# Five weight chunks of the mixer layer as ten chunks of 256 columns with two matmuls per tile, and ScalarE scaling the state-space output

## The reference, cut to what matters

```
proj = x @ w_in                                  # x: (256, 1024)
z, xbc, dt_raw = proj[:, :1024], proj[:, 1024:2560], proj[:, 2560:2576]
sc_b, sc_c, sc_h = the last three blocks of 1024 columns
xbc = silu(causal_dwconv(xbc, conv_w) + conv_b)  # 4 taps along the tokens
...                                              # scan over two blocks of 128 tokens, 16 heads
y_ssd = rms_norm_by_group(y * silu(z)) * norm_w  # 2 groups of 512 columns
y_sc  = sc_b * causal_dwconv(sc_c * sc_h, sc_conv_w)   # 3 taps
mix   = concatenate([y_ssd, y_sc]) @ w_out
```

## Time and profile before

| | |
|---|---|
| median of 3 runs | 1211.0 us (1210.92 to 1212.75) |
| the profiled execution, its own time | 1211.0 us |
| its span, first to last instruction | 1209.1 us |
| PE busy | 1202.8 us, 99% |
| PEld busy | 1043.0 us, 86% |
| DVE, ACT, POOL busy | 55%, 56%, 71% |
| the chain that ended last | PE 98% |
| granted TensorE clock | 1.000 |

### The profile page before, as it was taken

How to read it: one execution, slowest core, us unless ns; L and a number is a source line. 1 busy time by engine, 2 the same in 40 slices (tenths; PEclk the granted TensorE clock), 3 DMA queues, 4 the chain that set the end, 5 groups by cost and what they waited for, 6 DMA issues and landing times.

```text
span 1209.1 us, 18481 instructions
## 1 busy us (share of the span) xinstructions
PE 1202.8 (99%) x7352; PEld 1043.0 (86%) x7352; DVE 667.5 (55%) x1147; ACT 679.2 (56%) x913; POOL 855.8 (71%) x371
## 2 busy tenths in 40 slices
PE   9999999999999999999999999999999999999998
PEld 8987888888888888899999888888889878888887
DVE  6847546331256689646662255537753673544865
ACT  6873757655476755546544464445556666444543
POOL 7977468649978800968589788883776648998174
PEclk9999999999999999999999999999999999999999
DMA  9756355537656656746466766665657445666462
GB/s 303 214 161 174 107 155 157 157 89 222 211 151 197 190 164 217 215 130 192 124 178 216 251 200 189 182 197 164 224 147 279 140 121 173 186 202 189 160 223 70
DMA packets 147989, 218.32 MB, mean 181 GB/s; under 512 B 9792, under 2 KB 79808, under 8 KB 147904
## 3 DMA queue, kind: packets, MB, share of 16 engines
q1 hardware_dynamic: 144384, 209.92, 57.2%
q10 hardware_dynamic: 3520, 7.23, 1.7%
HBM read 216.08 MB, written 1.05 MB: 180 GB/s over the span
## 4 chain that ended last, share of the span: by engine, by line
PE 98%; DMA 0%; ACT 0%; DVE 0%; issue 0%; SPq 0%; DVEq 0%; ACTq 0%
PE acc L2285 18%; PE acc L2292 9%; PE acc L2322 9%; PE acc L2324 9%; PE acc L2323 9%; PE pm L2338 5%; PE acc L2329 4%; PE acc L2331 4%; PE acc L2332 4%; PE acc L2743 3%; PE acc L2744 3%; PE acc L2745 3%; PE acc L2251 2%; PE acc L2253 2%; PE acc L2252 2%; PE acc L2487 1%
## 5 line engine op out<-in xcount | busy, mean ns | idle before, releaser
L645 POOL TENSOR_TENSOR wlo<-raw,whi 128x1024 fp32r<-128x1024 f32 (+4 forms) x362 | 848.0, 2373 | 340.9 <-ACT whi L659 226.2
L659 ACT ACTIVATE whi<-raw 128x1024 fp32r<-128x1024 f32 (+4 forms) x404 | 403.7, 1022 | 210.9 <-PE acc L2292 54.0
L2285 PE MATMUL acc<-XT,whi 128*128 128x512 f32 x960 | 229.8, 391 | 0.4 <-DVE XT L1233 0.4
L2285 PEld LDWEIGHTS acc<-XT,whi 128*128 128x128 f32 x960 | 176.3, 188 | 35.2 <-issue 0.8
L2292 PEld LDWEIGHTS acc<-XT,wlo 128*128 128x128 f32 x960 | 123.4, 191 | 4.8
L2292 PE MATMUL acc<-XT,wlo 128*128 128x256 f32 x960 | 124.8, 283 | 0.0
L2322 PE MATMUL acc<-whi,XT 128*128 128x512 f32 (+4 forms) x296 | 112.5, 380 | 0.1
L2329 PE MATMUL acc<-XT,whi 128*128 128x256 f32 x392 | 111.7, 285 | 0.2 <-issue 0.2
L2331 PE MATMUL acc<-XT,whi 128*128 128x256 f32 x392 | 111.0, 283 | 0.0
L2332 PE MATMUL acc<-XT,wlo 128*128 128x256 f32 x392 | 111.0, 283 | 0.0
L2324 PE MATMUL acc<-whi,XT 128*128 128x512 f32 (+4 forms) x296 | 110.1, 372 | 0.0
(11 more groups left out here) (524 smaller groups left out, 2276.0 us busy)
## 6 DMA issues: line engine op xcount, KB each, us to landing
raw<-in_w_in SPq DMA_DIRECT2D x68, 512.0 KB, 3.9
raw<-in_w_ff SPq DMA_DIRECT2D x64, 512.0 KB, 3.8
raw<-in_w_gate SPq DMA_DIRECT2D x44, 512.0 KB, 3.8
raw<-in_w_up SPq DMA_DIRECT2D x44, 512.0 KB, 3.8
raw<-in_w_down SPq DMA_DIRECT2D x44, 512.0 KB, 3.9
raw<-in_w_in_mix SPq DMA_DIRECT2D x36, 512.0 KB, 3.8
raw<-in_w_branch SPq DMA_DIRECT2D x16, 512.0 KB, 3.8
raw<-in_w_out_mix SPq DMA_DIRECT2D x16, 512.0 KB, 3.4
```

The costliest lines, as they stand in the source:

```text
L645: nc.gpsimd.tensor_tensor(piece(wlo, u), piece(raw, u), piece(whi, u).bitcast(F32), ALU.subtract).then_inc(S["w_lo"], 1)
L659: return nc.scalar.activation(out_, in_, func, **k)
L2285: T.matmul(acc[:, n % 2, f, :], piece(whi, u)[:, i, f * P:(f + 1) * P], XT[:, :, k, :], start=k == 0, stop=False)
```

## The change

The chunks `xbc0`, `xbc1`, `sc1`, `sh1` and `sb1` are planned as ten "B" chunks of 256 columns, named `xbc00`, `xbc01`, `xbc10` and so on. The number of units stays the same. VectorE adds their partial sums in two new operations per chunk, the copy going into parts of the tile `em`. Each half is then convolved, multiplied and split by itself. At the start TensorE takes the first unit of `xbc01` between the two units of `xbc00`. ScalarE no longer copies `sc1`, VectorE's addition writes `scc`. The four scalings of `yd` go from VectorE to ScalarE, before the high halves of `sb0`'s result. The output products wait for their tiles by the finer count of `c_lo`.

```diff
+    def halves(name, at):
+        for h in range(2):
+            g.append((f"{name}{h}", "w_in_mix", KD, at + h * HW, HW, "B"))
...
-        g.append((f"xbc{c}", "w_in_mix", KD, M_XBC + c * W, W, "F"))
+        if c < 2:
+            halves(f"xbc{c}", M_XBC + c * W)
+        else:
+            g.append(("xbc2", "w_in_mix", KD, M_XBC + c * W, W, "F"))
...
-            g.append((f"{n}{c}", "w_in_mix", KD, o + c * W, W, "F"))
+            if c == 0:
+                g.append((f"{n}0", "w_in_mix", KD, o, W, "F"))
+            else:
+                halves(f"{n}1", o + W)
...
+        part_sums = em[:].rearrange("p h r s -> p h (r s)").rearrange("p h (f t) -> p h f t", t=TOK)
+        SHORT_OUT = (("sb0", slice(8, 12)), ("sb10", slice(12, 14)), ("sb11", slice(14, 16)))
...
 # ScalarE
-                act.wait_ge(*evac_at(f"xbc{j}"))
+                act.wait_ge(*evac_at(("xbc01", "xbc11", "xbc2")[j]))
...
-            for c in range(2):
-                if c:
-                    leave("sc1", scc[:])
-                high_halves(landed(f"sb{c}") + AHEAD)
-                act.wait_ge(S["c_out"], c + 1)
-                fn(BYhi[:, 8 + 4 * c:12 + 4 * c, :], accF(f"sb{c}"), ACT.Copy).then_inc(S["c_hi"], 1)
+            high_halves(landed("sb0") - 2 + AHEAD)
+            act.wait_ge(S["y_ss"], 2)
+            for k in range(4):
+                last = fn(y4[:, k, :], y4[:, k, :], ACT.Copy, scale=rs[:, k:k + 1])
+            last.then_inc(S["y_n"], 1)
+            for n, (name, tiles) in enumerate(SHORT_OUT):
+                high_halves(landed(name) + AHEAD)
+                act.wait_ge(S["c_out"], n + 1)
+                fn(BYhi[:, tiles, :], short_view(name), ACT.Copy).then_inc(S["c_hi"], 1)
...
 # VectorE
+            def parts_added(name, h, out_=None):
+                v.wait_ge(S["w_used"], landed(name))
+                link(V.tensor_copy(part_sums[:, h], accB(name, 1)))
+                return V.tensor_tensor(accB(name, 0) if out_ is None else out_, accB(name, 0), part_sums[:, h], ALU.add)
...
+            for j in range(3):
+                if j < 2:
+                    for h in range(2):
+                        link(parts_added(f"xbc{j}{h}", h))
+                        convolved(f"xbc{j}{h}", accB(f"xbc{j}{h}", 0), 4 * j + 2 * h)
...
-            for k in range(4):
-                last = V.tensor_scalar(y4[:, k, :], y4[:, k, :], rs[:, k:k + 1], None, ALU.mult)
-            last.then_inc(S["y_n"], 1)
-            short_output(0)
-            short_input(1)
-            short_output(1)
+            V.engine_nop().then_inc(S["y_ss"], 1)
+            v.wait_ge(S["w_used"], landed("sb0"))
+            short_output(0, "sh0", slice(0, 4))
+            for h in range(2):
+                parts_added(f"sc1{h}", h, scc[:, 2 * h:2 * h + 2]).then_inc(evac_at(f"sc1{h}")[0], 1)
+            for h in range(2):
+                v.wait_ge(*evac_at(f"sc1{h}"))
+                link(parts_added(f"sh1{h}", h))
+                short_input(f"sh1{h}", 1, slice(2 * h, 2 * h + 2))
+            for h in range(2):
+                link(parts_added(f"sb1{h}", h))
+                short_output(1 + h, f"sh1{h}", slice(2 * h, 2 * h + 2))
...
 # TensorE
-            product("xbc0", XThi, XTlo, 0, 1, ready=turned("x3"))
+            product("xbc00", XThi, XTlo, 0, 1, ready=turned("x3"))
             pe.wait_ge(*evac_at("f2_1"))
             turn("x3", X, first=2)
-            product("xbc0", XThi, XTlo, 1, ready=turned("x3"))
-            product("xbc1", XThi, XTlo)
+            product("xbc01", XThi, XTlo, 0, 1, used=0)
+            product("xbc00", XThi, XTlo, 1, ready=turned("x3"), used=2)
+            product("xbc01", XThi, XTlo, 1)
+            product("xbc10", XThi, XTlo)
+            product("xbc11", XThi, XTlo)
...
-            from_x("sc1")
-            from_x("sh1")
-            from_x("sb1")
+            for name in ("sc1", "sh1", "sb1"):
+                for h in range(2):
+                    from_x(f"{name}{h}")
...
-                product(name, BYhi[:, KD:], BYlo[:, KD:], start, stop, ready=lambda j: (S["c_lo"], j // 2 + 1))
+                product(name, BYhi[:, KD:], BYlo[:, KD:], start, stop, ready=lambda j: (S["c_lo"], max(1, j)))
```

More of the change, by code:

```diff
@@ L542, in accB, with short_view @@
             return acc[:, n % 2, 0:w // P, part * TOK:(part + 1) * TOK]
+        part_sums = em[:].rearrange("p h r s -> p h (r s)").rearrange("p h (f t) -> p h f t", t=TOK)
         f1s = pm[:, 3, :].rearrange("p (f t) -> p f t", t=TOK)
         hm = pm[:, 3, :].rearrange("p (f t) -> p f t", t=TOK)
+        y4 = yd[:].rearrange("p t (g d) -> p (t g) d", g=2)
+        SHORT_OUT = (("sb0", slice(8, 12)), ("sb10", slice(12, 14)), ("sb11", slice(14, 16)))
+        def short_view(name):
+            return accF(name) if chunks[name][5] == "F" else accB(name, 0)
         def last_gate(j):
@@ L991, in _ @@
             turn("x3", XThi, first=2)
-            high_halves(landed("xbc1") + AHEAD)
+            high_halves(landed("xbc11") + AHEAD)
             def silu2(j):
-                act.wait_ge(*evac_at(f"xbc{j}"))
+                act.wait_ge(*evac_at(("xbc01", "xbc11", "xbc2")[j]))
                 fn(xbcT[:, 4 * j:4 * j + 4, :], xbcT[:, 4 * j:4 * j + 4, :], ACT.Silu).then_inc(S["silu2"], 1)
@@ L1799, in by_head, with convolved @@
                 return ap.rearrange("p (h d) -> p h d", d=SSD_D)
-            for j in range(3):
-                v.wait_ge(S["w_used"], landed(f"xbc{j}"))
+            def parts_added(name, h, out_=None):
+                v.wait_ge(S["w_used"], landed(name))
+                link(V.tensor_copy(part_sums[:, h], accB(name, 1)))
+                return V.tensor_tensor(accB(name, 0) if out_ is None else out_, accB(name, 0), part_sums[:, h], ALU.add)
+            def convolved(name, view, first):
+                n = view.shape[1]
                 for back in range(4):
-                    for f in range(4 * j, 4 * j + 4):
-                        w, x = bcol("ssd_conv_w", 12 * (3 - back) + f), accF(f"xbc{j}")[:, f % 4, 0:TOK - back]
+                    for f in range(first, first + n):
+                        w, x = bcol("ssd_conv_w", 12 * (3 - back) + f), view[:, f - first, 0:TOK - back]
                         if back == 0:
@@ L1811, in _ @@
                         link(last)
-                last.then_inc(evac_at(f"xbc{j}")[0], 1)
+                last.then_inc(evac_at(name)[0], 1)
+            for j in range(3):
[3 more added lines that the diff above has]
+                        convolved(f"xbc{j}{h}", accB(f"xbc{j}{h}", 0), 4 * j + 2 * h)
+                else:
+                    v.wait_ge(S["w_used"], landed("xbc2"))
+                    convolved("xbc2", accF("xbc2"), 8)
                 if j == 1:
@@ L1854, in _, with short_input @@
             V.tensor_tensor(yd[:, 1, :], off, yd[:, 1, :], ALU.add).then_inc(S["s_yod"], 1)
[L1856 to L1861, removed]
+            def short_input(name, c, tiles):
+                gated = short_view(name)
+                link(V.tensor_tensor(gated, gated, scc[:, tiles], ALU.mult))
                 for back in range(3):
-                    for f in range(4):
+                    for f in range(tiles.start, tiles.stop):
                         w = bcol("sc_conv_w", 8 * (2 - back) + 4 * c + f)
-                        x = gated[:, f, 0:TOK - back]
+                        x = gated[:, f - tiles.start, 0:TOK - back]
                         if back == 0:
@@ L1872, in short_input, with short_output @@
                         link(last)
[L1873 to L1883, removed]
+                last.then_inc(evac_at(name)[0], 1)
+            def short_output(n, source, part):
+                name, tiles = SHORT_OUT[n]
+                view = short_view(name)
+                v.wait_ge(*evac_at(source))
+                V.tensor_tensor(view, view, scv[:, part], ALU.mult).then_inc(S["c_out"], 1)
+                v.wait_ge(S["c_hi"], n + 1)
+                V.tensor_tensor(BYlo[:, tiles, :], view, BYhi[:, tiles, :].bitcast(F32), ALU.subtract)\
+                    .then_inc(evac_at(name)[0], 1)
+                v.wait_ge(*evac_at(name))
                 V.engine_nop().then_inc(S["c_lo"], 1)
@@ L1923, in _ @@
             finished(3)
-            short_input(0)
+            v.wait_ge(S["w_used"], landed("sh0"))
+            v.wait_ge(*evac_at("sc0"))
+            short_input("sh0", 0, slice(0, 4))
             v.wait_ge(S["y_ss"], 1)
@@ L1927, in _ @@
             refine_columns(0, 4)
-            y4 = yd[:].rearrange("p t (g d) -> p (t g) d", g=2)
-            for k in range(4):
-                last = V.tensor_scalar(y4[:, k, :], y4[:, k, :], rs[:, k:k + 1], None, ALU.mult)
-            last.then_inc(S["y_n"], 1)
-            short_output(0)
-            short_input(1)
-            short_output(1)
+            V.engine_nop().then_inc(S["y_ss"], 1)
[10 more added lines that the diff above has]
+                short_output(1 + h, f"sh1{h}", slice(2 * h, 2 * h + 2))
```

## The result

The changed kernel takes 1213.9 us (median of 11 executions, 1212.21 to 1214.94), the one before, measured beside it, 1211.0 us (11 executions, 1210.8 to 1212.75). The ratio is 1.0022, interval 1.0014 to 1.0029: slower by about the 0.2% that the prediction took as the limit, and outside its range. The profiled execution of the changed kernel is among the shortest: its own time is 1212.66 us and its span 1210.8. Nine of the eleven took longer than 1213. So the trace shown first has 1.7 us of the loss, and the other 1.2 us up to the median are not in it.

What follows compares the result with a forecast made beforehand. TensorE's unbroken stream was taken as the bound; 1211.0 us − 1.95 (matmuls) + 2.75 (first evacuation) + 0.03 (thin margins) gave 1211.8 us, no change within 0.2%, with an overall range of 1209.0 to 1213.6.

Steps and rivals of the forecast that it cites:

- What bounds the kernel: TensorE, busy 99% at 2.4 GHz: savings in its stream and waits put before its matmuls count in full.
- The matmuls, −1.95 us: Five 512-column chunks as 256-column halves, two matmuls per tile instead of three: 0.39 us saved each, 1.95 us together.
- The first evacuation, +2.75 us: At xbc10, TensorE waits for VectorE to evacuate xbc00 with only 2.79 us of cover: a 2.75 us stall.
- the clock falls after the gap: Rival: after the stall, xbc10 runs at 1.2 GHz to its end, 1217.4 us; chance 12%.
- The later evacuations at nothing: Evacuations after xbc00's, through xbc, sh10, sc10, sc11 and sb10, are all covered; 0.03 us charged for thin margins.
- thin handovers: Rival: a half takes VectorE 5.4 instead of 5.11 us, first stall 3.05, dt waits 0.15; 1212.3 us; chance 8%.
- stretched copies: Rival: GpSimd stretches VectorE's copies to em by 1.2 us each, 1216.6 us; chance 3%.
- no wait: Rival: VectorE finishes a half in 2.5 us, so the gain stands alone, 1209.1 us; chance 9%.
- The scaling of `yd` at nothing: Four scalings, 6.6 us on VectorE, move to ScalarE at 2.5 us, off TensorE's path: no cost.

Runs made afterwards that it cites:

- The second half alone: Changed kernel with xbc0 and xbc1 left as three-matmul chunks; only sc1, sh1, sb1 halved and yd scaled on ScalarE: 1209.89 us, ratio 0.9989.
- with the DMAs moved as well: Changed kernel with acc released early, plus ScalarE's two attention-bias DMAs issued behind the halves of x6: 1209.31 us, ratio 0.9994.
- the changed kernel with the gap filled: Changed kernel plus unread 128x512 matmuls ahead of xbc10: with twelve 1212.07 us, with six 1211.9 us.
- the eleven with 1.79 us: Changed kernel plus three unread 128x512 matmuls ahead of xbc10, listed gap 1.79 us: 1213.6 us, ratio 1.0017.
- the 12 with 1.1 us: Changed kernel plus six unread 128x512 matmuls ahead of xbc10, listed gap 1.1 us: 1211.9 us, ratio 1.0005.
- the early release alone: Changed kernel with each xbc half's partial sums added into a pm bank, acc released right after, convolution reading pm: 1209.82 us, ratio 0.9988.

## Why the prediction was wrong

**What bounds the kernel** held: TensorE's stream set the time, and each wait put before a matmul came through to the end.

**The matmuls, −1.95 us**, held. The second half alone brought 1.14 of 1.17 us, the whole change without its gap 1.2 us, and 1.7 with the DMAs moved as well.

**The first evacuation, +2.75 us**, held: 2.64 us of wait and 0.15 by which TensorE came to it late. With the two terms the forecast of 1211.8 us is about the time of the changed kernel with the gap filled, 1212.07 and 1211.9 us. Left unfilled it took more even where the clock stayed up, 1212.7 us in the median of the ten executions at a mean clock of 1.000.

**The step that failed is the rival "the clock falls after the gap": its chance, and its price.** I gave it 12%, because 2.75 us seemed short beside full stretches of hundreds of microseconds on both sides. Since no row before had such a gap, that was no reading of a row. The runs show about one execution in two: of the 22 with the gap of 2.48 us the twelve with a mean clock below 1.000 took 1213.41 us and more, the ten others 1213.46 and less; of the eleven with 1.79 us seven are long; of the 12 with 1.1 us none; and all five of the kernel before with 2.55 us put in are long. The price was wrong too, in the other direction: I had the whole of `xbc10` at 1.2 GHz, +5.57 us and 1217.4 us in all. The clock came back within some 3 us, so it was 1.37 and 1.56 us in the two profiles that show it behind this gap, and 1.6 between the two groups. The prediction's condition, slower by over 0.2% from 1.6 us at the low level on, had the limit in the right place: the loss lies on it. Without any fall the median would have been near 1212.7, inside the range.

**The remaining 0.9 us**, 1212.7 against 1211.8, had no term in the sum. The first profile is an execution of 1212.66 us, and its ledger shows 0.6 of them as the wait at `aq0`, the rest as small steps. The second profile has 0.1 us at `aq0`. With the bias DMAs moved, ten of eleven executions lie within 0.75 us of each other, where eleven of the twelve with the early release alone spread over 1.2; that speaks for ScalarE's DMA issues as a cause of the spread. But it is not shown: the one profile of the version with the early release, an execution of 1209.59 us, has only 0.1 us at `aq0`, its longer executions were not profiled, and the two versions were not measured side by side. That part stays open.

**The later evacuations at nothing** held, in both profiles of the changed kernel: no wait at `dt`, `sb10`, `sb11` or `mo0a`. The rivals of thin handovers and of stretched copies are out (copy 0.69, half 5.09 us), and so is "no wait".

**The scaling of `yd` at nothing** held for the change as it is, but the reason I gave was half of it. I looked at the kernel before, where it lay in a full stretch, and not at what the new chunks leave of its cover. Kept on VectorE it costs a second gap of 3.0 us, and the median is 1217.3 us. The sum didn't suffer from it; an edit of the two without the other would have.

## What to carry to other kernels

Where TensorE runs without a break, price a new gap as its length plus a fall of the clock, here some 1.5 us in about half of the executions or more, behind listed gaps of 1.8 to 2.6 us; and look for the release that can be moved up (add the partial sums into a free bank and let the accumulator go) before accepting the gap. Cut a chunk in two, and the cover for everything that must be evacuated two places later halves too: go through each wait at `enter` with the new length, also those whose edit looks free. When a median lies above the profiled execution, the cause may not be in that trace: count the executions in groups, read the mean clock of each, and take a second profile.

## What the runs showed of the hardware

- A gap of 2.48 us brought the granted clock to 0.50 in one profile and left it at 1.00 in the other, in the same kernel with the same instructions before and after; by the mean clocks it fell in twelve of 22 executions at most. Listed gaps of 1.1 us were followed by no long execution in 12, of 1.79 us by seven in 11, of 2.55 us by five in 5. One of 2.99 us left the clock at 1.00 in the execution that was profiled.
- The low level lasted some 3 us behind the gap each time, with TensorE busy all the while: 522.5 to between 525 and 526, and 526 to 529.
- Four scalings of 128x512 in SBUF took VectorE 6.58 us. While GpSimd was writing `wlo` one took up to 2.62 us; the last of the four began after GpSimd had ended (626.3 against 626.07, and in the kernel before 622.4 against 622.23) and took 0.48. VectorE's operations with a source in PSUM kept their time (copy 0.69, tap operation 0.47).
- The time of one and the same DMA issue on ScalarE's queue varies: that of `b_v` took 1.17 and 0.51 us in the two profiles of the changed kernel, and 0.41 moved behind the halves of `x6`; that of `ln_mix_b` took 0.45 us before and 1.21 and 1.64 in the changed kernel.
